# Moving dense parts of a two-block transformer kernel: a second PSUM bank for a gate tile, gate parts ahead of the key spread, and three parts between the two value halves

## The reference, cut to what matters

```
# first block, per head h of 4 (written here without chunks)
scores = (k q^T) * decay                  # keys x queries, causal
sums   = column sums of scores            # the denominator
h      = (v^T scores) / max(|sums|, floor)
hm     = rmsnorm(h) * m_norm * sigmoid(m_o) * silu(m_z)   # m_o, m_z: dense projections

# second block, 16 heads in pairs
q = rope(rms_norm(q_lora @ w_uq));  k = rope(rms_norm(kv_lora @ w_ukv))
o = softmax(q k^T + causal) @ v
g = sigmoid(u @ w_gate + gate_b)          # 2 x 1024 columns: 16 dense tiles of 128
```

## Time and profile before

| | |
|---|---|
| median of 3 runs | 1721.95 us (1721.48 to 1721.99) |
| profiled execution, its time | 1719.81 us |
| profiled execution, its span | 1718.0 us |
| TensorE busy | 1638.5 us, 95% of the span |
| VectorE, ScalarE, GpSimd busy | 1047.3, 789.3 and 656.6 us |
| mean granted TensorE clock | 0.985 |
| memory attention | about 281 to 416 us of the span |
| latent loop | about 1026 to 1256 us of the span |

### The profile page before, as it was taken

How to read it: one execution, slowest core, us unless ns; L and a number is a source line. 1 busy time by engine, 2 the same in 40 slices (tenths; PEclk the granted TensorE clock), 3 DMA queues, 4 the chain that set the end, 5 groups by cost and what they waited for, 6 DMA issues and landing times.

```text
span 1718.0 us, 22325 instructions
## 1 busy us (share of the span) xinstructions
PE 1638.5 (95%) x7880; PEld 1290.4 (75%) x7899; DVE 1047.3 (61%) x1589; ACT 789.3 (46%) x1330; POOL 656.6 (38%) x307
## 2 busy tenths in 40 slices
PE   7999999999999799999997999999999999999999
PEld 6688777767887688666675887776778788888887
DVE  6599586676346676768786047777665555666200
ACT  5423465654253554666562245556543344444210
POOL 4244562323451344334352432222234344444442
PEclk9999999999998899999998999999999899999999
DMA  6243322223331333211111221211133233333331
GB/s 202 73 116 95 89 69 62 62 62 126 107 98 50 119 109 99 62 50 41 46 61 62 86 86 50 62 50 50 50 123 98 63 102 94 96 98 98 98 98 62
DMA packets 40118, 142.71 MB, mean 83 GB/s; under 512 B 4696, under 2 KB 5176, under 8 KB 39648
## 3 DMA queue, kind: packets, MB, share of 16 engines
q1 hardware_dynamic: 37600, 131.96, 25.5%
q10 hardware_dynamic: 2432, 9.59, 1.6%
HBM read 137.31 MB, written 4.21 MB: 82 GB/s over the span
## 4 chain that ended last, share of the span: by engine, by line
PE 79%; DVE 12%; ACT 6%; issue 3%; POOL 0%; ACTq 0%; DVEq 0%; POOLq 0%
PE bank L727 16%; PE bank L729 16%; PE bank L728 15%; PE bank L1313 4%; PE bank L1314 4%; PE bank L1312 4%; PE bank L1208 2%; PE bank L779 1%; PE bank L780 1%; PE bank L778 1%; PE bank L1229 1%; PE bank L1121 1%; PE bank L1217 1%; PE bank L748 1%; DVE xdec L2403 1%
## 5 line engine op out<-in xcount | busy, mean ns | idle before, releaser
L592 POOL TENSOR_TENSOR w_lo<-w_raw,w_hi 128x1024 fp32r<-128x1024 f32 x243 | 591.0, 2435 | 1021.2 <-ACT w_hi L1334 875.7
L727 PE MATMUL bank<-u_hi,w_hi 128*128 128x512 f32 x776 | 332.6, 429 | 17.3 <-DVE taps L2343 9.0
L1334 ACT ACTIVATE w_hi<-w_raw 128x1024 fp32r<-128x1024 f32 x199 | 209.1, 1055 | 222.7 <-PE bank L729 180.3
L729 PE MATMUL bank<-u_hi,w_lo 128*128 128x512 f32 x776 | 305.0, 393 | 0.0
L728 PE MATMUL bank<-u_lo,w_hi 128*128 128x512 f32 x776 | 304.4, 392 | 0.0
L727 PEld LDWEIGHTS bank<-u_hi,w_hi 128*128 128x128 f32 x776 | 146.8, 189 | 61.8 <-issue 14.6
L728 PEld LDWEIGHTS bank<-u_lo,w_hi 128*128 128x128 f32 x776 | 147.1, 190 | 33.6 <-issue 5.3
L729 PEld LDWEIGHTS bank<-u_hi,w_lo 128*128 128x128 f32 x776 | 146.6, 189 | 32.0
L1312 PE MATMUL bank<-u_hi,w_hi 128*128 128x512 f32 x320 | 124.5, 389 | 0.0
L1313 PE MATMUL bank<-u_lo,w_hi 128*128 128x512 f32 x320 | 124.5, 389 | 0.0
L1314 PE MATMUL bank<-u_hi,w_lo 128*128 128x512 f32 x320 | 124.5, 389 | 0.0
(11 more groups left out here) (462 smaller groups left out, 3443.8 us busy)
## 6 DMA issues: line engine op xcount, KB each, us to landing
w_raw<-weights SPq DMA_DIRECT2D x243, 512.0 KB, 3.6
xt<-x_t SPq DMA_DIRECT2D x8, 256.0 KB, 6.4
hank<-bias_dram ACTq DMA_DIRECT2D x8, 256.0 KB, 4.3
xt<-x_t ACTq DMA_DIRECT2D x1, 2048.0 KB, 9.3
h_dram<-h_res ACTq DMA_DIRECT2D x1, 2048.0 KB, 7.0
h_res<-h_dram ACTq DMA_DIRECT2D x1, 2048.0 KB, 7.5
out<-h_res SPq DMA_DIRECT2D x8, 256.0 KB
p_val<-p_t ACTq DMA_DIRECT2D x1, 512.0 KB, 11.4
```

The costliest lines, as they stand in the source:

```text
L592: pool.tensor_tensor(w_lo[:, j, :], w_raw[:, j, :], w_hi[:, j, :].bitcast(F32), ALU.subtract).then_inc(w_lo_ready, 1)
L727: pe.matmul(o, hi, xh, start=(i == 0), stop=False)
L729: mm = pe.matmul(o, lo, xh, start=False, stop=(i == n - 1))
L1334: act.activation(w_hi[:, c % RING, :], w_raw[:, c % RING, :], ACT.Copy).then_inc(w_hi_ready, 1)
```

## The change

Three edits, all in TensorE's order and in the banks.

1. `mix_gate` in the plan: gate tiles of even number from 2 on, the second of each pair, take bank 1, in which the queries are projected, instead of bank 0.
2. The latent loop: the gate parts of a step come ahead of `project_query(2p+2)` in step 0 and ahead of `key_spread` in step 4. In step 5 `head_logits(n + 3)` comes behind the gate parts.
3. Memory attention: the first three parts of `oz[4h+2]` come between the two value halves, ahead of the wait for `ml_added` and the sums; the other five stay where they were.

```diff
     def mix_gate(h, c):
-        plan.use_banks(0)
+        plan.use_banks(0 if h == 0 or h % 2 else 1)
         return plan.open("mix_gate", [(c, s) for s in range(KD)], [])
...
                 for v in range(2):
                     if v:
 
+                        column_tile(oz[4 * h + 2], of_u, part=(0, 3))
                         pe.wait_ge(ml_added, h + 1)
...
                     mm.then_inc(ml_values, 1)
-                column_tile(oz[4 * h + 2], of_u)
+                column_tile(oz[4 * h + 2], of_u, part=(3, KD))
                 column_tile(oz[4 * h + 3], of_u, part=(0, 4))
...
                 more = 2 * p + 2 < XH
-                if n + 3 < len(heads):
+                if i != 5 and n + 3 < len(heads):
                     head_logits(n + 3)
                 if more and i == 0:
                     project_keys(p + 1)
-                    project_query(2 * p + 2)
-                if more and i == 4:
-                    key_spread(p + 1)
                 if more:
                     column_tile(st["mix_gate"][2 * p + 1 + i // 4], of_u2, part=(i % 4 * 2, i % 4 * 2 + 2))
                 else:
                     column_tile(st["mix_gate"][2 * p + 1], of_u2, part=(i, i + 1))
+                if i == 5 and n + 3 < len(heads):
+                    head_logits(n + 3)
+                if more and i == 0:
+                    project_query(2 * p + 2)
+                if more and i == 4:
+                    key_spread(p + 1)
                 if more and i == 1:
```

## The result

The changed kernel takes 1730.66 us (median of four runs, 1729.71 to 1733.96) against 1721.72 us before: a ratio of 1.0056, with a 95% interval of 1.0039 to 1.0074. It is slower by 8.9 us. The profiled execution took 1730.63 us, with a span of 1728.8 us.

A forecast was written before the change was run, and what follows sets the result against it. TensorE, busy 95% of the span, was taken to bound the kernel, with memory attention one chain on VectorE and ScalarE. Memory attention +2.6 and loop +5.4 gave +8.0 us, 1730.0 us, range 1724.0 to 1736.0.

The forecast's parts named there:

- Memory attention, +2.6 predicted: Memory attention: parts ahead of the sums delay the VectorE and ScalarE chain, +2.6 us, bounds +2.0 and +3.4.
- The step that mattered: Timelines around TensorE's waits: a wait pays only if the work behind it is not waiting on a chain made later.
- The slack at L672: Squares' sum in memory attention: 0.77 us of slack, so TensorE arrives 1.4 us early and waits there.
- the term of heads 1 to 3: Memory attention's later heads: sums start 0.15 us later in each, 0.45 us together.
- The query behind the gate parts, +1.36 a pair: Loop steps 0 and 1: the later first query delays the second equally, +1.36 us in each of seven pairs.
- Steps 4 to 6, -0.6 a pair: Loop: waits for r_qk and gm go, but later keys leave 0.6 us gained a pair, bounds 0 and -1.6.
- The first pair, +1.4: Loop's first pair: lower clock in steps 3 and 4, so nothing credited back there, +1.4 us.
- The bank for nothing: Loop: moving gate 2p+2 to bank 1 costs nothing of its own.
- The last pair, -0.6: Loop's last pair: gate 15 no longer waits for gate 14's reader, -0.6 us, bounds 0 and -0.8.
- The clock: Rival: waits before the query sums lower the granted clock; 1734 us with falls in three more pairs, 1739 in all; chance 0.12.
- The port: Rival, loop step 4: GpSimd's subtraction beats VectorE's multiply, second head's keys 2.1 us later, 1742 us; chance 0.06.
- The rivals on the other side: Loop: keys no limit, 1722.2 us, chance 0.07; or VectorE late at neither hand-over, 1713 us, chance 0.06.

The follow-up runs named there:

- number 2: Kernel before with the memory attention edit in heads 1 to 3 only, head 0 in its old order: 1720.07 us, ratio 0.9997.
- number 6: Kernel before with only the plan's line changed (gate 2p+2 in bank 1), all orders as before: 1720.04 us, ratio 0.9997.
- number 5: Changed kernel without the memory attention edit and with project_query(2p+2) ahead of step 0's gate parts again: 1720.74 us, ratio 1.0000.
- number 7: As number 5, but one gate part of step 4 ahead of key_spread and one behind it: 1717.85 us, ratio 0.9992.
- number 12: Changed kernel with the key sums of step 2 moved between its two gate parts: 1728.53 us, ratio 1.0051.
- number 9: As number 7, but the key sums of step 2 moved between its two gate parts: 1714.55 us, ratio 0.9962.
- number 8: As number 4, but on VectorE head_keys(2p+3) comes right behind head_keys(2p+2): 1739.62 us, ratio 1.0113.
- number 4: Changed kernel without its memory attention edit, so the loop edits alone: 1727.68 us, ratio 1.0039.
- number 10: Kernel before with memory attention's sums from the four score tiles, ahead of both value halves, without VectorE's key_sum additions: 1716.52 us, ratio 0.9973.
- number 3: Kernel before with the memory attention edit, but six parts in place of three ahead of the sums: 1735.62 us, ratio 1.0082.

## Why the prediction came out right

**Memory attention, +2.6 predicted, +2.27 in the trace and 2.3 alone.** The step that mattered held: head 0 had no wait to fill, so the sums there came late by the parts' full length (2.17 us worked out, 2.13 measured), and the chain on VectorE and ScalarE carried that to `mix_lo`. The slack at L672 was 0.77 us, and a wait of 1.27 us stands there now, for 1.4 expected. Mis-sized was the term of heads 1 to 3: 3 x 0.15 us predicted, 0.07 in all measured in number 2 and 2.27 - 2.13 = 0.14 in the changed kernel.

**The query behind the gate parts, +1.36 a pair.** The distance between the two queries did not change by more than 0.01 us, and the wait is 1.18 us beside the 1.36 of the shift. A wait is counted from the recorded end of the matmul ahead, 0.39 us behind its start, and the next one could start 0.23 us behind it; by that estimate the wait hides another 0.16 us, 1.34 in all. In the first pair it is 2.40 us, as worked out. Taking the edit back gave 0.96 us, since the query then waits for the gate tile's reader instead.

**Steps 4 to 6, -0.6 a pair.** Both waits went, the spread came late, and VectorE's 5.3 us held. The wait for `k_s` is 1.05 us for 1.1 expected. By the pair's length the gain was 1.36 - 0.87 = 0.5 us. The steady pair cost +0.87 for +0.76 predicted. What the prediction did not see is how the gain divides: the bank alone brings 0.5 us a pair (number 6), one gate part ahead of the spread another 0.3, and the second takes 0.7 away (numbers 5 and 7).

**The first pair, +1.4.** It cost 32.63 - 30.62 = 2.0 us, with a stretch at the low clock in both kernels. The sum took steps 4 to 6 at nothing there, and the new wait for `k_s`, 1.06 us, stands in this pair too. How the 0.6 us beyond the sum divide was not worked out.

**The bank for nothing.** This held in the changed kernel, where the gate parts stand in front of the query. It is not free by itself: with the query first it costs a wait of 0.6 us for `gm` (number 5).

**The last pair, -0.6.** It gave 1.1, if the seventh pair is taken as a steady one: 49.30 - 31.15 = 18.15 us in number 12, against 49.51 - 30.27 = 19.24 before. The bound of 0.8 was too narrow; the rest of the pair was not walked through.

**The clock.** The rival that I gave 0.12 came true in part. Beside the one in the first pair, which before has as well, there were two stretches at the low clock in the loop, 1.6 us each, and one less behind the loop. Without these 3.2 us the loop cost 6.1 us for the 5.4 predicted. I had looked for the cause in the new waits. In number 12's trace the two are gone with the key sums set apart and the waits unchanged. The one in the first pair, at the wait of 2.40 us, stayed. What the prediction says of short idle spells stands in the Trainium skill's page TensorE: Matmul & The Clock Gate under "A second HAM failure mode: psum-queue depth-cycling", not under HAM oscillation. Numbers 9 and 12 speak against it as the only cause, since they keep the waits and have fewer falls.

**What was luck.** The mechanism held, and most of its terms, but not the closeness of 1730.0 to 1730.66. The profiled execution came out 10.8 us longer where the sum said 8.0, mostly by the two falls, which the sum did not have. The forecast added the 2.1 us by which the median of before lay above its profiled execution; the changed kernel's median lies at its profiled execution. These two errors nearly cancel. Before's medians in the experiments, 1720.1 to 1720.9, are also below the 1721.95 that the forecast started from.

**The port.** It did not happen, by the 0.5 us that I had put on it (1148.92 against 1148.40). Number 8 made such a collision happen, on the multiply in place of the keys.

**The rivals on the other side** needed the query's chain or the keys to leave slack. The rows of both hand-overs showed none, and the experiments agree.

## What to carry to other kernels

A wait of the busiest engine is only worth its length if the work behind it does not end at a wait on the same chain. Before filling one, walk on from it to the next hand-over in both directions, and look at the rounds of the loop in which the wait is not there: this edit filled three waits, gained nothing, and paid its full length in the one head that had none.

Where two engines hand something back and forth, shorten the chain and not the idle time. Here TensorE took on 4.8 us of work to spare VectorE a sum, and 4.3 us were won. And cover a wait with no more work than it is long: one part ahead of the key spread gained 0.3 us a pair, and the second one lost 0.7.

## What the runs showed of the hardware

In the loop the granted clock fell in stretches where TensorE was recorded as 100% busy, but for the fall at the wait of 2.40 us in the first pair. What stood ahead of them were matmuls with one or two columns, transposes and a few value matmuls, 2.4 us of them in a row. These are the matmuls of step 2 in the trace of before, from the key sums to the values:

```profile
1128.74 0.95 PE L1184 MATMUL bank<-in_half,sq_k 128*128 128x2 f32 x8
1129.55 1.03 PE L1176 MATMUL bank<-ones,sq_q 96*128 96x1 f32 x8
1130.44 0.41 PE L1217 MATMUL bank<-squares_f,probs_x 128*128 128x128 f32 x2
1130.78 0.44 PE L1229 MATMUL bank<-turned_x,v_tok 128*64 128x128 f32 x4
```

A fall cost 1.6 us in numbers 4, 5, 7 and 9 and in the changed kernel, and 0.9 in number 6, whose pairs with a fall have no wait for `r_qk`. In the second pair of number 10 it cost 0.3. The row is the same in every pair, and the fall is not. Which pairs it hit differed from kernel to kernel: one of the seven in before and in number 9, three in number 5, four in number 7, each counted in one execution. What decides it was not found. With three matmuls of 128x512 set between the two groups of sums, and no work added, one was left in number 9 and only the first pair's in number 12. Numbers 6 and 7 had more of them than before, and so they show little or no gain by their times, and 0.5 and 0.8 us a pair by their undisturbed pairs. The Trainium skill (TensorE: Matmul & The Clock Gate, HAM oscillation) describes a fall behind idle gaps; the falls of number 3, behind waits of 3.3 us, are of that kind. Those in the loop came in stretches without an idle gap, in pairs whose waits were 1.2 us or shorter, but for 2.4 us in the first pair and 2.0 in number 8.

GpSimd's subtraction of two SBUF tiles held up a VectorE multiply that reads and writes SBUF only (0.42 us became 1.48 in number 8, 0.49 became 2.67) and an addition of two SBUF tiles (0.29 became 2.39), each until it was over. VectorE's instructions that read PSUM ran beside it at their usual length: the last one of the keys took 0.68 us beside it in the changed kernel, and 0.68 without it before.
